# PEER stage: choice of candidates on lists in PSUM, expert grids 16 per 15 rows, first activation row in buffers of its own

## The reference, cut to what matters

```
q = (xt @ w_query).reshape(t, 8, 2, 64)
s = einsum('thkd,hknd->thkn', q, sub_keys)
vals, idx = top_k(s, 16)
cand = (vals[:, :, 0, :, None] + vals[:, :, 1, None, :]).reshape(t, 8, 256)
best, pos = top_k(cand, 16)
i1 = take_along_axis(idx[:, :, 0], pos // 16, axis=-1)
i2 = take_along_axis(idx[:, :, 1], pos % 16, axis=-1)
expert, gate = i1 * 128 + i2, softmax(best)
a = einsum('cd,ced->ce', xb, u_tab[expert])
out = einsum('ce,ced->cd', gate * gelu(a), v_tab[expert])
```

## Time and profile before

| | us |
|---|---|
| median of 3 runs | 1756.91 |
| lowest and highest | 1756.22, 1757.22 |
| the profiled execution | 1755.37 |
| its span, first to last instruction | 1753.6 |
| TensorE busy in it | 1656.9 (94%) |
| DVE, ACT, POOL busy | 910.8, 919.0, 1210.7 |
| mean granted TensorE clock, share of 2.4 GHz | 0.988 |

### The profile page before, as it was taken

One profiled execution on the slowest core, in us unless ns is written; L12 is line 12 of the kernel. 1 busy time (PEld: TensorE's weight loads), 2 busy tenths in 40 slices (PEclk: granted clock), 3 DMA queues, 4 the chain that ended last, 5 costly groups with the idle time before them and its releaser, 6 DMA issues.

```text
span 1753.6 us, 32136 instructions
## 1 busy us (share of the span) xinstructions
PE 1656.9 (94%) x12786; PEld 1509.6 (86%) x12786; DVE 910.8 (52%) x1875; ACT 919.0 (52%) x1541; POOL 1210.7 (69%) x500
## 2 busy tenths in 40 slices
PE   6988999999999999999999999989999998989997
PEld 5976999998999998777778888768999986789997
DVE  6978446993166666777721115866220067652101
ACT  5675655443544444555556666565553356556532
POOL 4552777899777777777788887215888861268885
PEclk9999999999999999999999999999999999999999
DMA  6431555555655555555556664513565644146563
GB/s 213 152 109 61 182 167 170 180 165 167 186 157 164 164 167 157 168 171 170 189 177 193 195 194 140 191 49 112 175 182 183 190 146 167 49 128 185 182 188 112
DMA packets 79604, 280.43 MB, mean 160 GB/s; under 512 B 8672, under 2 KB 9440, under 8 KB 79200
## 3 DMA queue, kind: packets, MB, share of 16 engines
q1 hardware_dynamic: 79456, 278.38, 50.6%
HBM read 277.30 MB, written 1.05 MB: 159 GB/s over the span
## 4 chain that ended last, share of the span: by engine, by line
PE 64%; DVE 3%; issue 2%; POOL 1%; ACT 1%; POOLq 0%; DVEq 0%; ACTq 0%
PE ps L2608 14%; PE ps L2004 12%; PE ps L2302 10%; PE ps L2615 7%; PE ps L2588 4%; PE ps L2589 3%; PE ps L2593 3%; POOL wl L199 1%; PE ps L2060 1%; PE ps L2574 1%; PE ps L2576 1%; PE ps L370 1%; PE ps L2126 1%; PE ps L2072 1%; PE ps L2065 1%
## 5 line engine op out<-in xcount | busy, mean ns | idle before, releaser
L199 POOL TENSOR_TENSOR wl<-slots,wh 128x1024 fp32r<-128x1024 f32 x236 | 570.7, 2421 | 379.1 <-ACT wh L184 363.1
L2410 POOL TENSOR_TENSOR wl<-slots,wh 128x1024 fp32r<-128x1024 f32 x256 | 635.3, 2485 | 147.9 <-ACT wh L2349 145.8
L2349 ACT ACTIVATE wh<-slots 128x1024 fp32r<-128x1024 f32 x256 | 271.3, 1060 | 389.6 <-issue 235.3
L184 ACT ACTIVATE wh<-slots 128x1024 fp32r<-128x1024 f32 x236 | 249.4, 1060 | 262.1 <-PE ps L2302 105.5
L2588 PE MATMUL ps<-xh,wh 128*128 128x256 f32 x1024 | 255.8, 288 | 0.9 <-ACT small L2386 0.9
L2589 PE MATMUL ps<-xl,wh 128*128 128x256 f32 x1024 | 250.4, 282 | 0.0
L2588 PEld LDWEIGHTS ps<-xh,wh 128*128 128x128 f32 x1024 | 195.5, 191 | 1.2 <-ACT small L2386 1.1
L2589 PEld LDWEIGHTS ps<-xl,wh 128*128 128x128 f32 x1024 | 195.9, 191 | 0.0
L2608 PE MATMUL ps<-wh,xh 128*128 128x512 f32 x512 | 163.8, 401 | 4.4 <-DVE xl L2524 4.4
L2608 PE MATMUL ps<-wh,xl 128*128 128x512 f32 x512 | 159.2, 392 | 0.0
L2593 PE MATMUL ps<-xh,wl 128*128 128x256 f32 x1024 | 144.4, 284 | 7.9 <-POOL wl L2410 7.8
(11 more groups left out here) (374 smaller groups left out, 3158.1 us busy)
## 6 DMA issues: line engine op xcount, KB each, us to landing
slots<-w SPq DMA_DIRECT2D x260, 512.0 KB, 3.5
slots<-wu SPq DMA_DIRECT2D x128, 512.0 KB, 3.5
slots<-wv SPq DMA_DIRECT2D x128, 512.0 KB, 3.5
arena<-bias SPq DMA_DIRECT2D x1, 2048.0 KB, 8.1
h<-xT SPq DMA_DIRECT2D x2, 512.0 KB, 5.5
arena<-keys SPq DMA_DIRECT2D x1, 1024.0 KB, 5.6
yT<-y_out SPq DMA_DIRECT2D x2, 512.0 KB, 2.7
layer<-consts SPq DMA_DIRECT2D x1, 800.0 KB, 5.1
```

The lines of the kernel that those rows point to most:

```text
L184: act.activation(self.hi[:, n % 2, :], self.slots[:, u % SLOTS, :], ACT.Copy).then_inc(self.rounded, 1)
L199: pool.tensor_tensor(self.lo[:, n % 2, :], self.slots[:, self.order[n] % SLOTS, :], self.hi[:, n % 2, :].bitcast(F32), ALU.subtract).then_ ...
L2349: act.activation(whv[:, r % 2, :], slots_v[:, r % SLOTS, :], ACT.Copy).then_inc(w_hi, 1)
L2410: pool.tensor_tensor(wlv[:, r % 2, :], slots_v[:, r % SLOTS, :], whv[:, r % 2, :].bitcast(F32), ALU.subtract).then_inc(w_lo, 1)
```

## The change

Three things change in PEER, and nothing outside it.

1. The lists `eq` and `sel` become one list `eq` in PSUM banks 4 and 5 (1024 elements), the lane numbers are copied to bank 6 first, and each of the four choices is done in two halves of four heads, with the multiply in place. A wait on `s_sel` keeps one choice behind the other.
2. `grids_ahead(row) = min(64, row * 16 // 15)` grids stand ahead of a row on TensorE, in place of row grids: rows 14, 29, 44 and 59 of a half get two, rows 60 to 63 none. DVE makes both kinds of one-hots of grid n before it spreads grid n - 1. In half 1 rest_a(row) stands in the pass n with grids_ahead(row) = n + 1, behind the spread.
3. Row 0 of A has buffers `row0_hi` and `row0_lo` (`std` and `rst` give up half of their columns for them). ACT does round_a(0) between up rows 126 and 127 and round_a(1) behind the last; DVE does rest_a(0) ahead of the first one-hots of half 1. The waits for `g_done` move into round_a(0) and round_a(64), and all round_a from row 2 on stand in one loop. TensorE's wait for `a_drained`, HALF moves into down_row(0).

```diff
--- before.py
+++ after.py
@@ -286,7 +286,8 @@
 
         xh, xl = sb("xh", DC * T, F32R), sb("xl", DC * T, F32R)
         wh, wl = sb("wh", 2 * SLOT, F32R), sb("wl", 2 * SLOT, F32R)
-        eps, std, rst = sb("eps", 4), sb("std", 512), sb("rst", 512)
+        eps, std, rst = sb("eps", 4), sb("std", T), sb("rst", T)
+        row0_hi, row0_lo = (sb(n, T, F32R)[:, :] for n in ("row0_hi", "row0_lo"))
         memory = ctx.enter_context(ExitStack())
         with nc.sbuf_tensor("early_hi", [P, DC * T], F32R) as early_hi, nc.sbuf_tensor("early_lo", [P, DC * T], F32R) as early_lo:
             pass
@@ -1324,8 +1325,12 @@
         keys_v = view(U + 2048, PH, T)
         cand = view(U, TT, PH, 256)
         s_v = view(U + 4096, TT, PH * 2, NSUB)
-        eq = view(U + 4096, PH * TOPK, TOPK)
-        sel = view(U + 6144, PH * TOPK, TOPK)
+        def grids_ahead(row):
+
+            return min(GROUPS, row * 16 // 15)
+
+        eq = ps[:, 2048:3072].rearrange("p (j n) -> p j n", n=TOPK)
+        iota16 = psum[6][:, 0:TOPK]
         f5 = arena[:, U + 8192:U + 8192 + 3456]
         idx = arena[:, U + 11648:U + 12160].bitcast(U32)
         vals = f5[:, 0:512].rearrange("p (t g n) -> p t g n", t=TT, n=TOPK)
@@ -1335,7 +1340,6 @@
         rank = f5[:, 1536:2048].rearrange("p (k t n) -> p k t n", k=2, t=TT)
         chosen = f5[:, 2048:2560].rearrange("p (k t n) -> p k t n", k=2, t=TT)
         gsum = f5[:, 2560:2576]
-        iota16 = const("lane")[:, 0:TOPK]
         ranku = f5[:, 2688:3200].bitcast(U32).rearrange("p (k n) -> p k n", k=2)
 
         per_slot = small[:, 0:768].rearrange("p (k t) -> p k t", k=3)
@@ -2356,12 +2360,14 @@
 
                 def round_a(row):
 
-                    if row >= 4:
-                        act.wait_ge(lo_done, NE2 + row - 3)
                     if row:
+                        act.wait_ge(lo_done, NE2 + max(0, row - 3))
                         act.wait_ge(e_lo, row)
+                    if row % HALF == 0:
+                        act.wait_ge(g_done, GROUPS * (row // HALF + 1))
                     act.activation(a_copy, A[:, row, :], ACT.Copy)
-                    act.activation(xhT[:, 4 + row % 4, :], A[:, row, :], ACT.Copy).then_inc(e_hi, 1)
+                    act.activation(row0_hi if row == 0 else xhT[:, 4 + row % 4, :], A[:, row, :],
+                                   ACT.Copy).then_inc(e_hi, 1)
 
                 first_act(act)
                 act.wait_ge(*ring.last[62])
@@ -2385,19 +2391,16 @@
                     act.wait_ge(s_tr, k + 1)
                     act.activation(per_slot[:, k], psum[4 + k][:, 0:T], ACT.Copy,
                                    scale=GATE_SCALE if k == 2 else 1.0).then_inc(s_slot, 1)
-                for r in range(HALF, NE2):
+                for r in range(HALF, NE2 - 2):
                     up_row(r)
-                act.wait_ge(lo_done, NE2)
-                for half in range(2):
-                    act.wait_ge(g_done, GROUPS * (half + 1))
-                    first = half * HALF
-                    round_a(first)
-                    round_a(first + 1)
-                    for row in range(first, first + HALF):
-                        if row + 2 < NE2:
-                            round_row(NE2 + row + 2)
-                        if row + 2 < first + HALF:
-                            round_a(row + 2)
+                up_row(NE2 - 2)
+                round_a(0)
+                up_row(NE2 - 1)
+                round_a(1)
+                for row in range(NE2):
+                    if row + 2 < NE2:
+                        round_row(NE2 + row + 2)
+                        round_a(row + 2)
                 layers_act(act)
 
             @block.gpsimd
@@ -2460,16 +2463,27 @@
                 dve.tensor_scalar(ranku[:, 0], posf, 4, None, ALU.logical_shift_right)
                 link(dve.tensor_scalar(ranku[:, 1], posf, 15, None, ALU.bitwise_and))
                 link(dve.tensor_copy(rank, ranku.rearrange("p k (t n) -> p k t n", t=TT)))
+                link(dve.tensor_copy(iota16, const("lane")[:, 0:TOPK]))
+                half = PH * TOPK // 2
                 for t in range(TT):
                     pair = idxf[:, t].rearrange("p (h k) n -> p h k n", k=2)
                     for k in range(2):
-                        link(dve.tensor_tensor(
-                            eq, bcast(rank[:, k, t, :], TOPK),
-                            iota16.rearrange("p (o n) -> p o n", o=1).broadcast_to([P, P, TOPK]), ALU.is_equal))
-                        place = pair[:, :, k, :].rearrange("p h (o n) -> p h o n", o=1).broadcast_to([P, PH, 16, 16])
-                        link(dve.tensor_tensor(sel.rearrange("p (h r) n -> p h r n", h=PH),
-                                               eq.rearrange("p (h r) n -> p h r n", h=PH), place, ALU.mult))
-                        dve.tensor_reduce(chosen[:, k, t, :], sel, AX.X, ALU.add).then_inc(s_sel, 1)
+                        if t + k:
+                            dve.wait_ge(s_sel, 2 * t + k)
+                        for g in range(2):
+                            slots16 = slice(g * half, (g + 1) * half)
+                            link(dve.tensor_tensor(
+                                eq, bcast(rank[:, k, t, slots16], TOPK),
+                                iota16.rearrange("p (o n) -> p o n", o=1).broadcast_to([P, half, TOPK]), ALU.is_equal))
+                            place = pair[:, g * PH // 2:(g + 1) * PH // 2, k, :]\
+                                .rearrange("p h (o n) -> p h o n", o=1).broadcast_to([P, PH // 2, 16, 16])
+                            by_head = eq.rearrange("p (h r) n -> p h r n", h=PH // 2)
+                            link(dve.tensor_tensor(by_head, by_head, place, ALU.mult))
+                            ins = dve.tensor_reduce(chosen[:, k, t, slots16], eq, AX.X, ALU.add)
+                            if g:
+                                ins.then_inc(s_sel, 1)
+                            else:
+                                link(ins)
                 dve.wait_ge(s_e5, 1)
                 link(dve.tensor_reduce(gsum, gate, AX.X, ALU.add))
                 link(dve.reciprocal(gsum, gsum))
@@ -2521,25 +2535,28 @@
                     dve.wait_ge(e_hi, row + 1)
                     if row >= 4:
                         dve.wait_ge(lo_done, NE2 + row - 3)
-                    dve.tensor_tensor(xlT[:, 4 + row % 4, :], a_copy, xhT[:, 4 + row % 4, :].bitcast(F32),
-                                      ALU.subtract).then_inc(e_lo, 1)
+                    hi, lo = (row0_hi, row0_lo) if row == 0 else (xhT[:, 4 + row % 4, :], xlT[:, 4 + row % 4, :])
+                    dve.tensor_tensor(lo, a_copy, hi.bitcast(F32), ALU.subtract).then_inc(e_lo, 1)
 
                 for half in range(2):
-                    dve.wait_ge(a_drained, HALF // 2 * (half + 1))
+                    if half:
+                        rest_a(0)
                     marks(half, 0)
                     gated_marks(half, 0)
+                    dve.wait_ge(a_drained, HALF // 2 * (half + 1))
                     if half:
                         dve.wait_ge(lo_done, NE2)
-                        rest_a(0)
                         rest_a(1)
+                    row = 2
                     for n in range(1, GROUPS):
                         marks(half, n)
+                        gated_marks(half, n)
                         spread(half, n - 1)
-                        gated_marks(half, n)
-                        if half and n + 1 < HALF:
-                            rest_a(n + 1)
+                        if half and grids_ahead(row) == n + 1:
+                            rest_a(row)
+                            row += 1
                     spread(half, GROUPS - 1)
-                for row in range(HALF, NE2):
+                for row in range(row, NE2):
                     rest_a(row)
 
                 layers_dve(dve)
@@ -2597,7 +2614,9 @@
 
                     r = NE2 + row
                     hi, lo = whv[:, r % 2, :], wlv[:, r % 2, :]
-                    a_hi, a_lo = xhT[:, 4 + row % 4, :], xlT[:, 4 + row % 4, :]
+                    a_hi, a_lo = (row0_hi, row0_lo) if row == 0 else (xhT[:, 4 + row % 4, :], xlT[:, 4 + row % 4, :])
+                    if row == 0:
+                        pe.wait_ge(a_drained, HALF)
                     pe.wait_ge(w_hi, r + 1)
                     pe.wait_ge(e_hi, row + 1)
                     pe.wait_ge(e_lo, row + 1)
@@ -2637,13 +2656,14 @@
                         ins = pe.transpose(psum[4 + k][:, t * P:(t + 1) * P], src, const("ident"))
                     ins.then_inc(s_tr, 1)
                 pe.wait_ge(s_slot, 3)
-                for r in range(HALF, NE2):
-                    up_row(r)
-                    grid(0, r - HALF)
-                pe.wait_ge(a_drained, HALF)
+                for row in range(HALF):
+                    up_row(HALF + row)
+                    for n in range(grids_ahead(row), grids_ahead(row + 1)):
+                        grid(0, n)
```

(3 more changed lines are left out.)

## The result

| | before | changed |
|---|---|---|
| median, us | 1756.89 (4 runs, 1756.22 to 1757.22) | 1742.64 (4 runs, 1742.25 to 1743.81) |
| profiled execution, us | 1755.37 | 1742.68 |
| its span, us | 1753.6 | 1740.9 |

The ratio is 0.992 (95% interval 0.9906 to 0.9935): 14.25 us faster, where 8.05 were forecast and the range ended at 1745.0. The direction was right, the size wrong.

What follows compares the result with a forecast made beforehand. TensorE, busy 94% of the span, was taken as the bound, so only its gaps could be won. -7.25 - 2.0 + 1.2 = -8.05 us took 1756.91 to 1748.9 us; range 1745.0 to 1752.5.

Steps and rivals of the forecast that it cites:

- Part 1: Choice of candidates: with lists in PSUM, DVE and POOL stop taking turns and TensorE's waits go; -7.25 us.
- 7.25 at most, since no more is idle there: Choice of candidates: upper bound on the gain, taken from TensorE's idle time from 340 to 420 us.
- Part 2: Hand-over from up to down rows, with grids moved ahead: TensorE then waits only for the last Gelu; -2.0 us.
- Part 3: Down rows: gap before row 64 goes, grids shift, but four new stalls cost 3.6 us; +1.2 us in all.
- Four stalls: Down rows: TensorE waits for rest_a placed behind the spread of a double grid's first grid; 0.9 us each.
- the four rows named: Down rows 15, 30, 45 and 60, where grids_ahead skips a count and rest_a was expected late.
- A: Down rows: the stalls are absent because something gives rest_a earlier; 1745.3 us, chance 0.10.
- B: Down rows: each double grid stalls the next row too, another 3.6 us; 1752.5 us, chance 0.12.
- C: Choice: POOL keeps taking turns, now 16 times, losing 12.2 us in place of 7.25; 1761.0 us, chance 0.04.
- D: Choice's waits go only in part, or the hand-over's wait moves elsewhere; 1751 to 1754 us, chance 0.06.
- The sum: Whole kernel: the three terms added, -7.25 - 2.0 + 1.2 = -8.05 us.
- My last paragraph: Signs of right or wrong in the profile; a granted clock other than 1.00 in PEER counted as wrong.

Runs made afterwards that it cites:

- e7: Changed kernel with the lane numbers left in SBUF, so is_equal reads two SBUF operands and writes to PSUM; 1744.17 us, ratio 0.9929.
- e3: Kernel before with only the choice of candidates moved to half-length lists in PSUM; 1746.81 us, ratio 0.9954.
- e9: e6 with TensorE's wait for the last Gelu moved to the first product into bank 3; 1741.22 us, ratio 0.9915.
- e6: Changed kernel with rest_a of rows 15, 30, 45 and 60 one pass earlier; 1739.84 us, ratio 0.9903.
- e12: Kernel before, unchanged, run once more for its profile; one execution of 1758.26 us.
- e1: Kernel before, unchanged, run again to see the scatter between executions; 1756.93 us, ratio 1.0005.
- e5: Changed kernel run again, unaltered, beside many runs of the kernel before; 1743.78 us, ratio 0.9926.
- e2: Kernel before with only the SBUF layout changed: std and rst halved, row 0 buffers added but unused; 1757.09 us, ratio 1.0012.
- e4: Changed kernel with the choice back on lists in SBUF, keeping the new order and row 0 buffers; 1754.04 us, ratio 0.9990.
- e11: Changed kernel with row 0 of A in the shared buffers again and twelve extra DVE subtractions before rest_a(0); 1753.95 us, ratio 0.9989.

## Why the prediction was wrong in size and right in its mechanisms

**Part 1, the mechanism right, the term too small.** DVE and POOL took turns because of two reads from SBUF (e7), and with at most one such read they do not (profile after, e3). The step that failed is "7.25 at most, since no more is idle there": an idle time of TensorE is no upper bound of what a wait costs. The term measured 9.2 us (e3), 2.0 more than the 7.25 of the forecast.

**Part 2, right.** -2.1 against -2.0 us. The Gelu is what is late next, 0.9 us behind the last up product. e9 removes it.

**Part 3, right, somewhat too dear.** Four stalls of 0.86, of which 0.05 come back in the next row, at the four rows named, no knock-on; the down rows grew by 0.8 us, where 1.2 was forecast. e6 gives 3.3 us back. Rivals A and B are refuted by the waits, C by the POOL rows, D by both.

**What no step held: the granted clock at the gaps.** The sum took a gap at its length, 1.82 us before row 64 and 2.62 at the hand-over, and put what the clock takes at nothing. In the profile of before both are followed by clock 1.00, so nothing in it warned; e12 shows the same program with 3.3 us more. With one low stretch of 1.6 us in an execution on average (5 in 5), and none in the profiled executions of the changed kernel, removing the gaps is worth about 1.6 us more than their length, an estimate from these few. My last paragraph named a clock other than 1.00 as a way to be wrong, without a price.

The times of all executions say the same of the kernel as a whole. Those of the unchanged kernel (61, of e1 and of the batches beside e1, e5 and e9) go with their mean granted clock: 1757.2 us on average at 0.987, 1756.3 at 0.988, 1754.9 at 0.989, by a straight line 1.16 us for 0.001. On average they take 1756.5 us at 0.9877, and the nine of the changed kernel (first and e5) 1743.4 at 0.9893. The difference in clock is then worth 1.8 us of the 13.1 between them, again an estimate. It covers the whole program, so it does not show that all of it comes from the two gaps.

**The sum again.** 9.2 + 2.1 - 0.8 = 10.5 us in PEER, plus 1.6 to 1.8 for the clock: 12.1 to 12.3, against 13.1 over all executions, 12.9 in e5 and 14.25 measured first. Of that first figure about 1 us is luck of samples of four executions each. **What stays open** is the rest of about 1 us, and what moves the first block. It ended 1.7 us earlier in the first profile of the changed kernel and 0.9 in e5; the three profiles of the unchanged program have it at 276.4 to 276.8, those of the others at 274.4 to 275.6, but e9 at 277.3. A gain of the kernel from the layout is ruled out by e2, and e3 has neither layout nor order in common with e4 but the same early start. The traces show that the clock has a part in it. The first block has four or five stretches at 0.50 in each of them, of 17.1 us together in twelve of the fourteen, 20.5 in e12 and 23.9 in e9, the latest of all. They do not stand at the same places: before and e1 have one near 64 and one near 122 us, the changed kernel has none there, one near 137, and a first one twice as long (6.8 us in place of 3.4, near 30 us). But e11 has them where e1 has, and its first block ends at 275.0, so the places alone do not tell its length. Whether this is scatter, or an edit anywhere in the program moves these stretches, was not settled.

## What to carry to other kernels

Price a wait of TensorE by the starts of its instructions before and after, not by its idle time, and a gap of about 1.8 us or more also with what the clock may take at it; several profiled executions of the kernel before show what one hides. When a helper engine has little over per unit of work, look for VectorE instructions that read two operands from SBUF beside GpSimd's, and move one operand to PSUM. When two loops are interleaved at a ratio, check each operation at the steps where the count jumps by two: the condition "one ahead" skips exactly there.

## What the runs showed of the hardware

- At waits of TensorE of 1.8 to 2.7 us the clock fell to 1.2 GHz in 7 of 13 cases, in the same program in one execution and not in another, at about 1.6 us each; at waits of up to 1.3 us never. In those 7 it fell from 0.1 us before to 0.8 us after TensorE began again; in the one wait of 7.5 us (e11) it fell within the wait, 4 us before its end.
- A DVE tensor_tensor that reads two operands from SBUF took turns with POOL's subtraction even though it wrote to PSUM: 3.16 us in place of 1.23 (e7).
- A wait of TensorE ahead of the low 128x256 products cost 0.25 us more than its idle time (e3).
